# Two layers on one core: the relative-position bias lines are built on 128 partitions, and sixteen modulation rows are spread differently over the column phases

## The reference

```python
def hybrid_layer(x, c, rel_table, w_ada, ...):             # first layer
    mod = silu(c) @ w_ada + b_ada                          # 2048 -> 3 * 2048
    shift, scale, gate = split(mod, 3)
    h = rmsnorm(x, pre_g) * (1 + scale) + shift
    q, k, v, gate_a, u, gate_p = split(h @ w_in)           # 1024, 256, 256, 1024, 1024, 1024 columns
    y_a = windowed_gqa(q, k, v, rel_table, sink) * silu(gate_a)
    y_p = multiscale_pool(u, w_pool_grp, pool_scale) * silu(gate_p)
    g_a, g_p = split(sigmoid(h @ w_merge + b_merge))
    o = (g_a * (y_a @ w_br_attn) + g_p * (y_p @ w_br_pool)) @ w_out
    return x + gate * rmsnorm(o, post_g)

def windowed_gqa(...):                                     # 8 heads
    rel = key_pos - query_pos
    logits = q @ k.T * 128 ** -0.5 + rel_table[t5_bucket(rel)]   # a bias that depends on rel and head alone
    logits = where(abs(rel) <= 128, logits, -1e30) ...
```

## Time and profile before

| | us |
|---|---|
| median of 3 runs | 2468.97 |
| lowest and highest of the 3 | 2466.52, 2469.60 |
| the profiled execution | 2464.08 |
| its span in the profile | 2462.3 |
| TensorE busy in it | 2275.7 (92%) |
| TensorE's granted clock, mean over the span | 0.957 of full |

### The profile page before, as it was taken

How to read it: one execution, slowest core, us unless ns; L and a number is a source line. 1 busy time by engine, 2 the same in 40 slices (tenths; PEclk the granted TensorE clock), 3 DMA queues, 4 the chain that set the end, 5 groups by cost and what they waited for, 6 DMA issues and landing times.

```text
span 2462.3 us, 31231 instructions
## 1 busy us (share of the span) xinstructions
PE 2275.7 (92%) x12866; PEld 1973.4 (80%) x12866; DVE 1740.3 (71%) x2018; ACT 1119.5 (45%) x1417; POOL 74.2 (3%) x96
## 2 busy tenths in 40 slices
PE   3459999999998899999999989898999999999998
PEld 2348888888887778888888878787888888888887
DVE  6937868776877668776777788877777777774443
ACT  2123346664545464443455543455444444444443
POOL 0000000000000000000011110000000000000000
PEclk7579999999999999999999999999999999999999
DMA  9877787877885656668877778984555555565553
GB/s 383 308 211 270 257 280 258 295 263 241 286 310 169 223 190 210 232 217 278 300 250 235 249 268 312 327 292 140 188 188 188 188 185 184 184 218 184 174 187 104
DMA packets 245633, 580.55 MB, mean 236 GB/s; under 512 B 12266, under 2 KB 15134, under 8 KB 241268
## 3 DMA queue, kind: packets, MB, share of 16 engines
q1 hardware_dynamic: 232608, 535.93, 63.3%
q0 software_dynamic: 11696, 40.20, 5.3%
q10 hardware_dynamic: 1188, 2.44, 0.3%
HBM read 557.55 MB, written 20.97 MB: 235 GB/s over the span
## 4 chain that ended last, share of the span: by engine, by line
PE 78%; DVE 11%; DMA 7%; ACT 2%; issue 1%; ACTq 0%; SPq 0%; DVEq 0%
PE gemm L1720 45%; PE gemm L1721 23%; DVE w_lo L1068 3%; PE gemm L1724 3%; DMA mod_stage<-in_w_ada 3%; DMA w_stage<-in_w_ada 2%; DMA mod_stage<-in_w_mod 2%; DVE mod_acc L1062 2%; PE gemm L1723 1%; PE extra L1520 1%; PE extra L1513 1%; DVE mod_acc_scale L1046 1%; ACT w_hi L704 1%; PE extra L1652 1%; PE extra L1628 1%
## 5 line engine op out<-in xcount | busy, mean ns | idle before, releaser
L1720 PE MATMUL gemm<-operand_main,w_hi 128*128 128x512 f32 x4311 | 1563.2, 404 | 73.0 <-DVE proj L1394 27.1
L1721 PE MATMUL gemm<-operand_main,w_lo 128*128 128x256 f32 x4311 | 1218.9, 283 | 0.0
L1068 DVE TENSOR_TENSOR w_lo<-w_stage,w_hi 128x1024 fp32r<-128x1024 f32 x736 | 861.1, 1212 | 447.9 <-ACT w_hi L704 447.5
L704 ACT ACTIVATE w_hi<-w_stage 128x1024 fp32r<-128x1024 f32 x736 | 732.1, 1044 | 784.1 <-PE gemm L1721 704.3
L1720 PEld LDWEIGHTS gemm<-operand_main,w_hi 128*128 128x128 f32 x4311 | 822.2, 191 | 265.1 <-DVE w_lo L1068 60.7
L1721 PEld LDWEIGHTS gemm<-operand_main,w_lo 128*128 128x128 f32 x4311 | 826.0, 192 | 13.5
L1062 DVE SCALAR_TENSOR_TENSOR mod_acc<-mod_stage,c_silu,mod_acc 128x1024 f32<-128x1024 f32 x210 | 267.1, 1300 | 51.2 <-DMA mod_stage<-in_w_mod 40.0
L1720 PE MATMUL gemm<-ffn_hidden,w_hi 128*128 128x512 f32 x688 | 242.9, 397 | 0.0
L1721 PE MATMUL gemm<-ffn_hidden,w_lo 128*128 128x256 f32 x688 | 192.5, 280 | 0.0
L1720 PE MATMUL gemm<-operand_attn,w_hi 128*128 128x512 f32 x480 | 177.6, 410 | 14.5 <-DVE proj L1394 10.0
L1720 PEld LDWEIGHTS gemm<-ffn_hidden,w_hi 128*128 128x128 f32 x688 | 129.1, 188 | 29.5
(11 more groups left out here) (212 smaller groups left out, 1468.4 us busy)
## 6 DMA issues: line engine op xcount, KB each, us to landing
w_stage<-in_w_in SPq DMA_DIRECT2D x128, 1024.0 KB, 5.9
mod_stage<-in_w_mod SPq DMA_DIRECT2D x192, 512.0 KB, 5.9
w_stage<-in_w_up SPq DMA_DIRECT2D x88, 1024.0 KB, 5.0
w_stage<-in_w_down SPq DMA_DIRECT2D x44, 1024.0 KB, 5.0
w_stage<-in_w_merge SPq DMA_DIRECT2D x32, 1024.0 KB, 5.5
w_stage<-in_w_out SPq DMA_DIRECT2D x32, 1024.0 KB, 7.7
w_stage<-in_w_ada SPq DMA_DIRECT2D x31, 1024.0 KB, 7.5
mod_stage<-in_w_ada SPq DMA_DIRECT2D x32, 512.0 KB, 5.9
```

The lines of the kernel that those rows point to most:

```text
L704: return nc.scalar.activation(o, i_, f, **kw)
L1068: tt(WL[:, slot_of(n), c0:c1], WST[:, slot_of(n), c0:c1], WH[:, n % HIS, c0:c1].bitcast(F32), ALU.subtract)\
L1720: mm(G[:, m, :], hi, x_of(k), start=(k == 0), stop=False)
L1721: ins = mm(G[:, m, T:2 * T], lo, x_of(k)[:, 0:T], start=False, stop=False)
```

## The change

The eight lines are made on all 128 partitions: for each head ACT spreads its table column over 128 columns (`table_wide`), TensorE multiplies it with the one-hot matrix (the same line in every one of 128 output rows), and ACT copies the 128 x 512 result into `line_rows`, which now lies in the space of `operand_attn`. The store to `lines` then takes each of the 128 copies from a partition of its own, with the partition as its outer dimension. The rows of part 2 no longer run in `u0` and `u1`, but three to a phase from `in` 1 on, with the last in `gate_p1`, and `mod_end(2)` moves from behind `in_gates` 1 to behind `gate_p1`. The rows of part 3 run two to a phase in all eight `merge` phases.

```diff
-        LINE8 = proj_tile("line_rows", [HEADS1, LINE], F32, 52)
+        TABB = proj_tile("table_wide", [33, P], F32, 51)
+        LINEB = at("line_rows", [P, HEADS1, LINE], F32, o_opa)
...
-        phases.append(Phase("u0", 0, [one(2560)], mod=(2, 0, 2), slots=(0, 2)))
-        phases.append(Phase("u1", 0, [one(3072)], mod=(2, 2, 2), slots=(0, 2)))
+        phases.append(Phase("u0", 0, [one(2560)]))
+        phases.append(Phase("u1", 0, [one(3072)]))
         for n, c in enumerate((512, 1024, 1536)):
-            phases.append(Phase("in", n + 1, [one(c)], mod=(2, (4, 6, 8)[n], (2, 2, 3)[n]), slots=(0, 2, 1), hooks=pool(n)))
+            phases.append(Phase("in", n + 1, [one(c)], mod=(2, 3 * n, 3), slots=(0, 2, 1), hooks=pool(n)))
         for i in range(2):
-            phases.append(Phase("in_gates", i, [one(2048 + 1536 * i)], mod=((2, 11, 3), (2, 14, 2))[i],
-                                hooks={} if i else pool(3), post=[("mod_end", 2)] if i else []))
-        phases.append(Phase("gate_p1", 0, [one(4096)], mod=(3, 0, 2), slots=(1, 2), post=[("silu1", 0), ("v1", 0)]))
+            phases.append(Phase("in_gates", i, [one(2048 + 1536 * i)], mod=((2, 9, 3), (2, 12, 3))[i],
+                                hooks={} if i else pool(3), post=[]))
+        phases.append(Phase("gate_p1", 0, [one(4096)], mod=(2, 15, 1), slots=(1,), post=[("mod_end", 2), ("silu1", 0), ("v1", 0)]))
...
-                                mod=(3, 2 + 2 * i, 2) if i < 6 else (3, 8 + i, 1), slots=(0, 2) if i < 6 else (0,),
+                                mod=(3, 2 * i, 2), slots=(0, 2),
...
-            pool.wait_ge(line_copied, 1)
-            pool.dma_start(lines[:, 0:P * LINE].rearrange("h (q k) -> h q k", q=P),
-                           LINE8[:, :].unsqueeze(1).broadcast_to([HEADS1, P, LINE])).then_inc(start["lines_stored"], 16)
+            pool.wait_ge(line_copied, HEADS1)
+            pool.dma_start(lines[:, 0:P * LINE].rearrange("h (q k) -> q h k", q=P), LINEB[:, :, :]).then_inc(start["lines_stored"], 16)
...
-                        act.wait_ge(line_mm, 1)
-                        activate(LINE8[:, :], X[0][0:HEADS1, :], ACT.Copy).then_inc(line_copied, 1)
+                        act.wait_ge(start["line_in"], 32)
+                        for h in range(HEADS1):
+                            positive(act, line_mm, h)
+                            activate(TABB[:, :], TABX[:, h:h + 1].broadcast_to([33, P]), ACT.Copy).then_inc(line_col, 1)
+                            act.wait_ge(line_mm, h + 1)
+                            activate(LINEB[:, h, :], X[h % 2][:, :], ACT.Copy).then_inc(line_copied, 1)
                         split_hi(0)
...
-            mm(X[0][0:HEADS1, :], TABX[:, :], OHOT[:, :], start=True, stop=True).then_inc(line_mm, 1)
+            for h in range(HEADS1):
+                pe.wait_ge(line_col, h + 1)
+                if h >= 2:
+                    pe.wait_ge(line_copied, h - 1)
+                mm(X[h % 2][:, :], TABB[:, :], OHOT[:, :], start=True, stop=True).then_inc(line_mm, 1)
...
                 pe.wait_ge((half_row, mod0_rows)[half], (1, MOD0_ROWS)[half])
+                if half:
+                    pe.wait_ge(line_copied, HEADS1)
```

More of the change, by code:

```diff
@@ L454, in build @@
         vec_t, vec_copied, c_ready = sem("vec_transposed"), sem("vec_copied"), sem("c_ready")
-        line_mm, line_copied = sem("line_mm"), sem("line_copied")
+        line_col, line_mm, line_copied = sem("line_col"), sem("line_mm"), sem("line_copied")
         sq_ready, sq_used, sum_ready, x3_read, rs_ready = sem("sq_ready"), sem("sq_used"), sem("sum_ready"), sem("x3_read"), sem("rs_ready")
```

## The result

| | before | after |
|---|---|---|
| median of the runs taken together | 2469.28 (4 runs) | 2431.52 (4 runs) |
| lowest and highest | 2466.52, 2474.49 | 2428.56, 2438.84 |
| the profiled execution | 2464.08 | 2428.56 |
| its span | 2462.3 | 2426.8 |
| TensorE's granted clock, mean over the span | 0.957 | 0.967 |

After is 0.9849 of before, with a 95% interval of 0.9822 to 0.9876. That is 37.8 us between the medians and 35.5 us between the two profiled executions.

The account below looks back on a forecast made before the run. TensorE, busy 92% of the span, was taken as the bound, losing time in stops in the two pool-column phases. From 2469.0, -35.6 + 3.6 - 3.6 + 1.2 = -34.4 gave 2434 us, range 2424 to 2448.

Parts of the forecast that it names:

- The store: Store of `lines` from 128 partitions: near the 11.1 us of the store of x, landing by about 145 us.
- the sum from rows: Both stores, 4.2 MB at 387 GB/s, taking two thirds of the traffic, are through by about 141 us.
- the sentence on turns: Engines take turns between queues, so beside the store the slabs keep some 190 of 387 GB/s.
- The stops of `u0` and `u1` and the clock behind them: Pool-column phases: TensorE stops of 21.5 and 8.9 us go, plus 2.6 us of slower clock each, -35.6 us.
- The rows and the store as two chains: In `u0` and `u1`, late rows ahead of DVE's work and late slabs could each alone stop TensorE.
- the store stays slow: Rival: DRAM pieces of 2 KB set the store's pace, 17.8 us less gained, 2452 us; chance 0.12.
- The prologue: Eight heads at 2.0 us, loop from 37.8 to about 54 us, cost 0; cover gone over 6 us a head.
- Four phases with three rows: `in` 1, 2, 3 and `in_gates` 0: late evacuations and one slow clock stretch of 1.6, +3.6 us.
- Three rows are dear: Rival: all four pool phases cost 4.6 us each, 13.8 in place of 3.6, 2445 us; chance 0.15.
- `mod_end(2)` behind `gate_p1`: TensorE works in the 1.4 us wait and comes later to the 2.2 us one in `merge` 0, -3.6 us.
- `merge` 6: One more row of part 3 behind `poolmix` makes the evacuation 2.4 us later, +1.2 us.
- late pool weights: Rival: a very slow store delays the pool weights for `pool_sum` in `in` 1, 2485 us at most; chance 0.03.

Follow-up runs that it names:

- e8: The changed kernel measured again without any edit, 2436.8 us, 0.9864 of before.
- e10: The changed kernel measured a third time without any edit, 2432.8 us, 0.9851 of before.
- e3: Kernel before with the new row placement, its old store reading 8 source partitions four apart instead of neighbouring ones; 2426.6 us.
- e4: Kernel before with the new row placement, its store reading 16 neighbouring source partitions, 64 copies from each; 2445.2 us.
- e5: Changed kernel with the prologue's loop over the heads gone through twice, making the same eight lines twice; 2443.8 us.
- e6: Changed kernel with three rows of part 2 in `u1` and two in each pool phase; 2426.2 us.
- e9: The same kernel as e6 measured again, 2430.0 us, 0.9837 of before.
- e7: Changed kernel with `mod_end(2)` behind `in_gates` 1 again, the rows of part 3 as before and one row of part 2 in `u1`; 2435.9 us.

## Why the prediction was right

The forecast was 34.4 us less; 35.5 in the profiled executions and 37.8 in the medians were measured. All 13 executions of the changed kernel have a mean of 2434.1 us, where 2434 was said. Step by step, measured in the profiled execution of after, with `e8` and `e10` beside it where they differ:

- **The store.** It was to land by 145 us, I reckoned with 141; it landed at 141.1 (123.4 + 17.7). DMA share 1.0 until then, and TensorE without a wait up to 177 us. From 135 to 139.5 us the records have 317 packets of the store (4 KB each) and 307 of the loads (2 KB each): the two get nearly as many packets each, so the store gets 275 GB/s and the slabs 133. That is the two thirds of the sum from rows, and less for the slabs than the 190 of the sentence on turns. What I had put first as the cause, eight engines that carry the transfer alone, was the lesser one: `e3` and `e4` show that the eight neighbouring source partitions slowed each packet to 564 ns, and that the eight engines are worth a factor of two behind that. The number didn't depend on it, since the change removes both.
- **The stops of `u0` and `u1` and the clock behind them.** -35.6 predicted, -35.5 measured. No clock under 1.00 from `u1` to the end of `merge` 0 in this execution.
- **The rows and the store as two chains.** Right: the store alone brings 26.1 us, the rows alone 6.4. But the rival "the store stays slow" was priced at 2452 and a kernel in that state takes 2463 (2457.5 in the profile). It had slab 8 5.6 us too early, and the order on DVE was missing, evacuation behind the next `w_lo`.
- **The prologue.** Cost 0 predicted. 0.6 us were lost by the end of `in` 0, but the four profiles without the loop end it at 131.5 to 132.9 us and the eight with the single loop at 132.1 to 133.3, so that it costs anything is not shown. The working was wrong by half: 2.95 us a head for 2.0, the loop's end at 60.9 for 54, since I took the product's duration from a row at the full clock. The statement that the cover lasts up to 6 us a head is refuted by `e5`: its 16 rounds amount to 5.8 us a head and are 6.9 us over, so the cover ended at about 5 us a head.
- **Four phases with three rows.** +3.6 predicted, +1.1 measured, but +2.7 in `e8` and +3.4 in `e10`. The lateness was 0.2, 2.5, 1.2 and 1.4 us for my 1.5, 1.5, 2.3 and 1.3, and no stretch of slow clock followed, for which I had 1.6; in `e10` two of the four phases had it (0.93). So the first profile was a cheap one, and the term was better than it looks there. "Three rows are dear" is refuted: nothing near 4.6 us in each phase. `e6` and `e9` show that these waits come from the third row, as assumed. The windows of `in` 2 and `in_gates` 0 in `e10`:

```profile
204.45:230.22 25.77, 25.77 (x137) 22.45 (x138) 21.61 (x23) 7.11 (x8) 0.00 (x0) 0.93 0.78 257
...
256.80:282.86 26.06, 25.92 (x137) 22.42 (x137) 22.84 (x25) 7.45 (x9) 0.00 (x0) 0.93 0.78 281
```

- **`mod_end(2)` behind `gate_p1`.** From `in_gates` 1 to the start of `merge` 1 the lead grew from 33.8 to 38.4 us (78.1 us before, 73.4 after). The two waits gone are 3.6 of it (1.41 and 2.21 us), as predicted, and `e7` brings both back. The prediction also moved the slower clock behind `mod_end(2)` along, at no gain. In this execution it did not come: `gate_p1`, at 0.94 before, and `merge` 0 both ran at 1.00, which is worth 1.1 to 1.4 us. In every other profile the clock is down behind `mod_end(2)` (0.76 to 0.89 over the 12 us that follow), and `e8` and `e10` gain 3.7 and 4.2 us here, where this execution gained 4.7. So up to 1 us of the 38.4 is luck of this execution.
- **`merge` 6.** +1.2 predicted, 0.5 measured.
- **Behind 560 us** the sum had nothing. The lead first stays at 38 to 40 us, then 4 us of it go again in the second layer without any instruction there having changed. In `e8` and `e10` 8.3 and 7.5 us go behind `merge` 1, against the same one trace of before, which lies 4.9 us under its median. One pair of rows shows how the clock takes part of it back; the whole 4 us were not taken apart. Before:

```profile
1386.31 0.47 PE L1720 MATMUL gemm<-operand_main,w_hi 128*128 128x512 f32 x1 [2.51 <-DVE gate_out L1400]
...
1386.73 0.40 PE L1720 MATMUL gemm<-operand_main,w_hi 128*128 128x512 f32 x1
```

After, the same place:

```profile
1348.74 0.77 PE L1724 MATMUL gemm<-operand_main,w_hi 128*128 128x512 f32 x1 [2.51 <-DVE gate_out L1404]
...
1349.52 0.63 PE L1724 MATMUL gemm<-operand_main,w_hi 128*128 128x512 f32 x1
```

The same stop of 2.51 us is followed by matmuls at the full clock in one execution (0.40 us) and at the lower level in the other (0.63 us). So this forecast came out closer to the first profile than its parts deserve: the four phases, `mod_end(2)` and `merge` 6 were together 4.3 us cheaper there than I said, and the second layer took about as much. That these cancel is luck, and so is how near it lies to the medians, since the clock alone moves single executions by several us.

The price of the rival "late pool weights" was added up wrongly: +20 us on 2469.0 are 2489, not 2485. Nothing else rests on it.

## What to carry to other kernels

When a transfer is slow while the DMA share stands near a half, look at which partitions it reads: here a store from eight neighbouring partitions was cured by spreading the same eight lines four partitions apart, for one more small copy, as well as by building the data on all 128. The share alone does not tell it, since slabs alone show 0.52 too; 77 GB/s at that share do. A slow transfer that shares engines with the weight stream delays every slab behind it, so it costs where TensorE waits and not where it was issued. In this kernel the same three rows of optional work cost 8.4 us of TensorE's time in `u0`, beside the stores and the loads released by them, and nothing in `u1`, the phase behind, even though the two phases look alike in every other way. When a small term is read from a profile, take a second profile of the same kernel: here +1.1 us in one were +3.4 in another.

## What the hardware showed that was not expected

- The executions of the changed kernel spread over 10 to 11 us on one chip (2428.56 to 2438.84 in the first runs, 2431.55 to 2442.49 in `e8`). In the first runs the mean granted clock goes with it, 0.967, 0.964, 0.965 and 0.961 for 2428.56, 2430.79, 2432.25 and 2438.84 us; in `e8` only loosely (0.964 for 2436.81, 0.962 for 2431.55). The length of a stop of TensorE did not decide what followed: behind 2.50 and 3.25 us in `e8` the whole next phase had the clock 1.00, behind 2.04 and 2.24 us in `e10` it had 0.93. An estimate of a few us for clock stretches is thus no better than that spread.
- The product of 33 rows with 512 columns costs TensorE nearly the same for 8 output rows and for 128 (1.02 us and 1.09 us, both at the full clock), and 2.07 us at the lower level.
- Two transfers on the same engines got nearly as many packets each, 317 of the store and 307 of the loads in 4.5 us, and not as many bytes: with 4 KB against 2 KB in a packet the store got twice as much.
- Eight neighbouring source partitions did not keep DMA engines idle, they made each packet slow: 564 ns for 4 KB, against 159 from eight partitions four apart.
